# A constant of the tanh moves into the dot, the diagonals for TensorE are half filled ahead of the dot, and the engine of each weighing is chosen at the dot

## The reference

```
s1, i1 = top_k(sc[:, :, 0], 16);  s2, i2 = top_k(sc[:, :, 1], 16)
top_s, pos = top_k(s1[:, None] + s2[None, :], 16);  eid = take(i1 * 128 + i2, pos)
gate = softmax(top_s)
act  = gelu(einsum('cd,chkd->chk', h, u[eid]))            # one dot of 1024 for each token and expert
out  = einsum('chk,chkd->cd', gate * act, v[eid])         # 8 heads x 16 experts = 128 rows of v for each token
```

## Time and profile before

| | |
|---|---|
| median of 3 runs | 3405.8 us (3389.3 to 3409.6) |
| profiled execution, its own time | 3413.8 us |
| its span, first to last instruction | 3412.0 us |
| busy: TensorE / DVE / ACT / GpSimd | 2464.4 / 2574.2 / 1843.8 / 1300.2 us |
| moved by DMA | 1262.32 MB, of it 1086.39 MB by GpSimd's queue |
| granted TensorE clock, mean | 0.842 of full speed |

### The profile page before, as it was taken

The page is one execution under the profiler, slowest core; times in us unless marked ns, Lnnn a source line. Parts: engine busy times, 40 slices in busy tenths (PEclk is TensorE's granted clock), DMA queues, the critical chain, the costliest instruction groups (busy, mean ns, idle before and its releaser), DMA issues.

```text
span 3412.0 us, 34746 instructions
## 1 busy us (share of the span) xinstructions
PE 2464.4 (72%) x7098; PEld 1267.7 (37%) x7098; DVE 2574.2 (75%) x6105; ACT 1843.8 (54%) x6883; POOL 1300.2 (38%) x1044
## 2 busy tenths in 40 slices
PE   7967757898876688877777789868686622666676
PEld 4534434444433344433334344334332200233221
DVE  1267788888978878888778887787876586888854
ACT  1245564455666545566576554556566443455564
POOL 0023343333334534444444433334343344433453
PEclk8988867998976789999886799989898855787899
DMA  7979998899989999999999999999899999898998
GB/s 272 331 308 384 407 352 333 353 408 374 388 345 382 363 376 413 411 403 381 370 369 364 364 397 374 393 373 388 355 386 382 372 364 361 337 385 359 389 407 330
DMA packets 191360, 1262.32 MB, mean 370 GB/s; under 512 B 24849, under 2 KB 32873, under 8 KB 46737
## 3 DMA queue, kind: packets, MB, share of 16 engines
q0 software_dynamic: 149760, 1086.39, 79.7%
q1 hardware_dynamic: 41384, 173.70, 13.6%
HBM read 1251.24 MB, written 43.37 MB: 379 GB/s over the span
## 4 chain that ended last, share of the span: by engine, by line
DMA 30%; PE 25%; DVE 24%; ACT 6%; issue 6%; DVEq 4%; POOL 3%; ACTq 1%; SPq 1%; POOLq 0%
DMA uv_ring<-in_peer_uv,idx 23%; PE acc L1649 12%; DVE uv_ring L2283 9%; DVE accs L2290 5%; POOL uv_ring L1379 3%; PE pS L1438 3%; DMA o_all<-in_cache_swa 2%; PE pS L1557 2%; PE pA L1580 2%; DMA wbuf<-zS_scr 2%; ACT bent L1897 2%; ACT wv L1899 1%; PE acc L1438 1%; PE pS L1490 1%; ACT diag L1699 1%
## 5 line engine op out<-in xcount | busy, mean ns | idle before, releaser
L1379 POOL DMA_INDIRECT uv_ring<-in_peer_uv,idx x1024 | 1283.4, 1253 | 2070.4 <-PE acc L1649 1419.8
L1649 PE MATMUL acc<-uv_ring,diag 128*128 128x512 f32 x2456 | 1338.6, 691 | 493.8 <-ACT diag L1699 479.8
L2283 DVE SCALAR_TENSOR_TENSOR uv_ring<-uv_ring,hb 128x1024 f32<-128x1024 f32 x1032 | 1238.2, 1221 | 368.3 <-DMA uv_ring<-in_peer_uv,idx 348.6
L1649 PEld LDWEIGHTS acc<-uv_ring,diag 128*128 128x128 f32 x2456 | 507.5, 218 | 1169.2 <-ACT diag L1699 611.4
L1884 ACT ACTIVATE cube<-dots 128x1 f32<-128x1 f32 x1032 | 203.5, 197 | 970.9 <-DVE uv_ring L2283 960.5
L2290 DVE SCALAR_TENSOR_TENSOR accs<-uv_ring,wv,accs 128x1024 f32<-128x1024 f32 x410 | 526.7, 1285 | 63.4 <-ACT wv L1899 24.5
L1899 ACT ACTIVATE wv<-bent,half 128x1 f32<-128x1 f32 x1032 | 399.0, 387 | 74.4 <-issue 3.5
L1897 ACT ACTIVATE bent<-dots,line,cube 128x1 f32<-128x1 f32 x1032 | 398.8, 386 | 74.1 <-issue 2.8
L1699 ACT ACTIVATE half<-dots,gates 128x1 f32<-128x1 f32 x1024 | 286.6, 280 | 4.0 <-DVE gates L2175 4.0
L1580 PE MATMUL pA<-T,wbuf 128*128 128x256 f32 (+2 forms) x1280 | 259.4, 360 | 26.3 <-ACT sc L1699 16.1
L1699 ACT ACTIVATE diag<-idn,wv 128x128 f32<-128x128 f32 x614 | 246.5, 401 | 52.0 <-issue 2.1
(11 more groups left out here) (259 smaller groups left out, 2127.3 us busy)
## 6 DMA issues: line engine op xcount, KB each, us to landing
wbuf<-in_w_q SPq DMA_DIRECT2D x40, 1024.0 KB
out_dil_s<-in_cache_dil SPq DMA_DIRECT2D x8, 4092.0 KB
wbuf<-in_w_in SPq DMA_DIRECT2D x26, 1024.0 KB
wbuf<-in_w_out SPq DMA_DIRECT2D x20, 1024.0 KB
uv_ring<-in_peer_uv,idx POOLq DMA_INDIRECT x1024
uv_ring<-in_w_in SPq DMA_DIRECT2D x6, 1024.0 KB, 17.5
keysT<-in_keys SPq DMA_DIRECT2D x40, 128.0 KB
T<-in_xT_all SPq DMA_DIRECT2D x8, 512.0 KB, 13.2
```

The source lines that it names most:

```text
L1379: pool.indirect_dma_start(uv_ring[:, entry % RING, :], None, peer_uv, bass.IndirectOffsetOnAxis(rows, 0))\
L1649: m = pe.matmul(acc[0:R, side * 512:(side + 1) * 512], w, uv_ring[:, entry % RING, D + side * 512:D + (side + 1) * 512], start=first, stop ...
L2283: dve.scalar_tensor_tensor(row, row, 1.0, h, ALU.mult, ALU.mult, accum_out=dots[:, e % RING:e % RING + 1]).then_inc(u_dot, 1)
```

## The change

The dot is multiplied by C at once, so `line` falls away and x itself is the tanh's bias; CUBE and the gates' constant (0.5 becomes 0.5 / C) are adapted. For picks of TensorE, ACT writes identity * gate into the diagonal ahead of the dot ("seed"), the weight is then wv = x * bent + x without `half`, and the diagonal is multiplied by it in place. There are 6 diagonals in place of 4, and the wait for `v_pe` moves from "diag" to "seed". In the planner: the engine of the weighing is chosen when the dot is placed and no longer at the gate's end; "diag" no longer waits for an older weighing, "seed" does, for the one six back; a TensorE pick's gate waits for its seed; the costs and PE_BIAS are other numbers.

```diff
-CUBE = math.sqrt(0.044715 * GELU_C)
+CUBE = math.sqrt(0.044715) / GELU_C
...
-LINES = {"PE": ("weigh",), "ACT": ("gate", "diag", "final"), "DVE": ("weigh", "final", "dot")}
-URGENT = {"gate": 0.4, "diag": 0.5, "weigh": 0.6, "final": 0.7, "dot": 1.0}
+LINES = {"PE": ("weigh",), "ACT": ("gate", "diag", "seed", "final"), "DVE": ("weigh", "final", "dot")}
+URGENT = {"gate": 0.4, "seed": 0.55, "diag": 0.5, "weigh": 0.6, "final": 0.7, "dot": 1.0}
-PE_BIAS = -2.0
+PE_BIAS = -1.0
-GATE = 1.35
+GATE_PE, GATE_DVE = 1.15, 1.45
+DIAGS = 6
...
+                if self.on_pe[p] and u[0] == "f":
+                    return max(self.ends["seed", p], self.ends["dot", p]) if ("seed", p) in self.ends else None
...
+                older = [q for q in sorted(self.on_pe) if self.on_pe[q] and q < p][-DIAGS:1 - DIAGS]
+                if older and len([q for q in self.on_pe if self.on_pe[q] and q < p]) >= DIAGS:
+                    if ("weigh", older[0]) not in self.ends:
+                        return None
...
-            if p not in self.on_pe:
-                self.share(p, gate)
...
             if kind == "diag":
-                older = [q for q in sorted(self.on_pe) if self.on_pe[q] and q < p][-4:-3]
-                if older and ("weigh", older[0]) not in self.ends:
-                    return None
-                return max([gate] + [self.ends["weigh", q] for q in older])
+                return gate
...
+                if kind == "dot":
+                    self.share(p, at + time + GATE_PE)
...
+            def seed(p):
+
+                i = PE_ORD[p]
+                g = gate_of(pick_u(p))
+                if i >= DIAGS:
+                    act.wait_ge(v_pe, i - DIAGS + 1)
+                copy(diag[:, i % DIAGS, :], idn[:, :], g)
+
             def pick_gate(p):
...
+                seeded = ON_PE[p] and u[0] == "f"
                 act.wait_ge(u_dot, e + 1)
                 act.activation(cube[:, c], x, ACT.Square, scale=CUBE)
-                copy(line[:, c], x, GELU_C)
...
+                if not seeded:
+                    copy(half[:, c], x, gate_of(u))
                 act.drain()
-                act.activation(bent[:, c], x, ACT.Tanh, scale=cube[:, c], bias=line[:, c])
+                act.activation(bent[:, c], x, ACT.Tanh, scale=cube[:, c], bias=x)
                 act.drain()
-                act.activation(wv[:, c], bent[:, c], ACT.Identity, scale=half[:, c], bias=half[:, c]).then_inc(g_w, 1)
+                by = x if seeded else half[:, c]
+                act.activation(wv[:, c], bent[:, c], ACT.Identity, scale=by, bias=by).then_inc(g_w, 1)
...
-                if i >= 4:
-                    act.wait_ge(v_pe, i - 3)
-                copy(diag[:, i % 4, :], idn[:, :], w).then_inc(d_set, 1)
+                copy(diag[:, i % DIAGS, :], diag[:, i % DIAGS, :], w).then_inc(d_set, 1)
...
-                dve.scalar_tensor_tensor(row, row, 1.0, h, ALU.mult, ALU.mult,
+                dve.scalar_tensor_tensor(row, row, GELU_C, h, ALU.mult, ALU.mult,
                                          accum_out=dots[:, e % RING:e % RING + 1]).then_inc(u_dot, 1)
```

More of the change, by code:

```diff
@@ L544, in pick_line @@
         if k == "gate":
-            return [("gate", p, GATE) for p in places]
+            return [("gate", p, GATE_DVE) for p in places]
+        if k == "seed":
+            return [("seed", p, 0.42) for p in places if pick_u(p)[0] == "f"]
         return [(kind, t, time) for t in finals for kind, time in
@@ L606, in ready_pick @@
                 at = self.part_end.get((n, len(times_of(BASE[n])) - 1))
+                if self.on_pe[p] and u[0] == "f":
+                    return max(self.ends["seed", p], self.ends["dot", p]) if ("seed", p) in self.ends else None
                 return None if at is None else max(at, self.ends["dot", p])
+            if kind == "seed":
+                if p not in self.on_pe:
+                    return None
+                if not self.on_pe[p]:
+                    self.pick[e, line] += 1
+                    continue
+                u = pick_u(p)
+                n = self.given["g", u[1] // P, u[1] % P // TOPK]
+                at = self.part_end.get((n, len(times_of(BASE[n])) - 1))
+                older = [q for q in sorted(self.on_pe) if self.on_pe[q] and q < p][-DIAGS:1 - DIAGS]
+                if older and len([q for q in self.on_pe if self.on_pe[q] and q < p]) >= DIAGS:
+                    if ("weigh", older[0]) not in self.ends:
+                        return None
+                    at = None if at is None else max(at, self.ends["weigh", older[0]])
+                return at
             if kind == "fsum":
@@ L728, in plan @@
                 kind, p, time = self.picks[e, what][self.pick[e, what]]
+                if kind == "dot":
+                    self.share(p, at + time + GATE_PE)
+                if kind == "gate" and self.on_pe[p] and pick_u(p)[0] == "f":
+                    time = GATE_PE
                 self.pick[e, what] += 1
@@ L848, in build @@
         gates = sb("gates", [P, SLOTS, P])
-        diag = sb("diag", [P, 4, P])
+        diag = sb("diag", [P, DIAGS, P])
         idn = sb("idn", [P, P])
@@ L888, in build @@
         cube = sb("cube", [P, RING])
-        line = sb("line", [P, RING])
         half = sb("half", [P, RING])
@@ L1646, in weigh @@
                 else:
-                    w, R = diag[:, PE_ORD[p] % 4, :], P
+                    w, R = diag[:, PE_ORD[p] % DIAGS, :], P
                 for side in range(2):
@@ L1876, in sample_pT, with gate_of @@
                 copy(s_pTn[0:8, :, :], pT[0:8, 192:320].rearrange("p (s n) -> p s n", s=2)).then_inc(s_bTe, 1)
+            def gate_of(u):
+                if u[0] == "s":
+                    if u[1] == 0:
+                        act.wait_ge(sx_in, 32 * HEADS)
+                    return gateT[:, u[1]:u[1] + 1]
+                t, col = u[1] // P, u[1] % P
+                act.wait_ge(r_gate, GATED[t, col // TOPK])
+                return gates[:, SLOT[t], col:col + 1]
+            def seed(p):
[4 more added lines that the diff above has]
+                copy(diag[:, i % DIAGS, :], idn[:, :], g)
             def pick_gate(p):
@@ L1922, in _ @@
                 if what != "stage":
-                    {"gate": pick_gate, "diag": spread, "fsq": final_squares}[what](s)
+                    {"gate": pick_gate, "seed": seed, "diag": spread, "fsq": final_squares}[what](s)
                     continue
@@ L2174, in gate @@
                 D_()
-                return dve.scalar_tensor_tensor(out, gexp[0:R, c, :], 0.5, gsum[0:R, c].unsqueeze(2)
+                return dve.scalar_tensor_tensor(out, gexp[0:R, c, :], 0.5 / GELU_C, gsum[0:R, c].unsqueeze(2)
                                                 .broadcast_to([R, n, TOPK]), ALU.mult, ALU.mult)
```

## The result

The changed kernel takes 3357.8 us in the median of 4 runs (3350.1 to 3361.8), before 3407.4 us in as many; the ratio is 0.9858 with a 95% interval of 0.9823 to 0.9893, so 1.4% less. The forecast was 3369 us. The profiled execution's own time is 3350.1 us, 63.7 us less than that of before.

What follows compares the result with a forecast made beforehand. Late diagonals, caused by the written order, were taken as the limit, leaving DMA time unused. Order 45 us plus gate 8 us, seeds and choice 0, times 0.7 gave 37 us off 3405.8: 3369 us, range 3326 to 3418.

Steps and rivals of the forecast that it cites:

- What bounds the kernel: Gathers: diagonals filled late by the written order leave about 5% of DMA time, 160 us of 3200, unused.
- Part 1, the gate: ACT's gate: 0.28 us shorter for TensorE picks, 0.10 us for DVE picks; 8 us taken, between 6 and 33.
- the factor 0.7: On the sum of gate and order gains: in three of ten cases another late engine becomes the next wait.
- Part 2, the seeds: ACT: 602 new operations ahead of the dots' ends, mostly covered by waits; 0 taken, up to 9 us loss.
- Part 3, the order: ACT's order: later picks' gates between `wv` and fill fall 354 to 230, 35% of 130 us: 45 us.
- Part 4, the choice: Engine chosen at the dot: 314 picks change engine; 0 taken, 30 us kept both ways for the range.
- (a): Rival at the gathers: the DMA is the bound and nothing moves, 3406 us; chance 0.22.
- (c): Rival on ACT: gates tied to seeds waiting for TensorE stop the ring, slower at 3442 us; chance 0.10.
- (d): Rival: TensorE's late diagonals become late weighings of DVE, eating the gain, about 3395 us; chance 0.12.
- (b): Rival: late diagonals matter more, 54% holds and nothing replaces them, 78 us gain, 3328 us; chance 0.14.
- The signs: Profile after: TensorE's `diag` wait about 300 us, POOL's for TensorE about 1300, DMA share 0.96, ACT busy about 1718.

Runs made afterwards that it cites:

- e4_cost: The kernel before with the planner's gate cost 1.15 instead of 1.35, its choice of engines held fixed, no operation changed: 3361.7 us, ratio 0.9868.
- e1_fold: The kernel before with only the constant moved into the dot and `line` removed; order, choice of engines and four diagonals as before: 3394.0 us, ratio 0.9962.
- e2_ops: All operations of the changed kernel in the order and with the engine choice of the kernel before, each seed directly ahead of its gate: 3399.7 us, ratio 0.9978.
- e3_order: The changed kernel's order, engine choice and six diagonals with the operations of the kernel before (`line`, `half`, no seeds): 3361.8 us, ratio 0.9864.
- e9_next: The kernel before, its operations, engine choice and gate cost kept, with every diagonal fill placed directly behind its own gate: 3325.3 us, ratio 0.9769.
- e10_dve: The kernel before with gate cost 1.15 for DVE's picks alone, 1.35 kept for TensorE's, choice of engines held fixed: 3422.6 us, ratio 1.0054.
- e8_choice_b: The kernel before with the changed kernel's choice of engines held fixed, gate cost 1.35 kept, order planned anew: 3446.3 us, ratio 1.0103.
- e5_first: The changed kernel with every diagonal fill placed directly behind its own gate, engines chosen as the changed kernel does: 3319.2 us, ratio 0.9749.
- e12_simple: e9_next plus e1_fold: every fill right behind its gate, constant in the dot, no `line`, four diagonals, no seeds: 3323.4 us, ratio 0.9726.
- e13_seeds: e9_next plus e2_ops: every fill right behind its gate, with all operations of the changed kernel and six diagonals: 3319.7 us, ratio 0.9730.

## Why the prediction was right, and where it was not

**What bounds the kernel: right.** Late diagonals leave the DMA without work. Read from two stretches and the table of waits before the run, it held in the experiments: with the fills prompt the rate goes from 376 to 387 GB/s, with them later it falls to 371.

**Who makes them late: wrong.** The prediction said that the planner held the fills back until a weighing four picks older had ended. That rule holds nothing back: the planner of before writes the same order with a rule on four or on six picks back, or with none. What decides is the gate's cost. The planner spaces the dots of picks that lie ready by 1.31 (the cost of "dot" in `pick_line`), and with a gate of 1.35 the next gate is always due when one ends, ahead of the fill, which is due HOP = 0.15 later. With 1.15 there is room for the fill. The planner shows both steps when e4_cost's kernel is planned with other costs: at 1.309 there are 45 fills behind two or more gates and at 1.31 there are 85; at 1.159, just below 1.31 - 0.15, there are 175 later gates ahead of fills and at 1.16 there are 296. In the changed planner a cost of 1.35 for TensorE's gates, all else as changed, gives 391 later gates and not 230. That the number makes the order and the order the time is shown by e4_cost. The forecast did not suffer from this mistake, by luck: its counts, 354 and 230, were taken from the written orders, whoever made them. On the chip the next dot often comes later than in the plan, and ACT, which runs in order, waits for it with the fill behind it.

**Part 1, the gate.** `bent` starts 0.26 us after `cube` for a seeded pick (944.90 to 945.16 in the timeline), as worked out. The term was 8 us, 6 after the factor 0.7. e1_fold, with the smaller part of the cut alone, gave 13 us, e2_ops with all of it 8 us, with intervals as wide as the difference. In the changed kernel's order all the operations together gave 2 us (e3_order against the changed kernel). The term stands within what can be measured.

**Part 2, the seeds: right** in that they cost nothing on the path, and this is why they win nothing: they remove 0.18 us more from a gate and add an operation of 388 ns.

**Part 3, the order: right mechanism, sized too low.** 45 us x 0.7 = 32 us were forecast, e3_order gave 1.36% of 3407 = 46 us, and e4_cost, without the new choice, 1.32% = 45 us. That the sum of the forecast came near owes something to the cut of 0.7: the same price, 130 us for all the later gates, gives 67 us for e4_cost, which removes 52% of them, and 130 us for e9_next, which gave 79 us. There the factor fits, 0.67 and 0.61; for the changed kernel it was not needed. The number of later gates is a rough measure, and the fills behind two or more are no better one: e10_dve and e8_choice_b have fewer of these than before and are slower.

**Part 4, the choice: 0 taken.** With before's costs and an order planned around it, it costs 1.0% or 35 us, a little over the 30 us that were kept; in the new order it may win up to 0.5%.

**The rivals.** (a), the DMA as the bound: the limit of about 358 GB/s from HBM that the Trainium skill gives in "DMA: Bandwidth & Descriptors", section "Where 436 GB/s comes from", does not hold for this core, which moves 384 GB/s as the mean of 3100 us and 387 in e9_next. Its reads from HBM alone are 1251 MB by the page of the changed kernel, 374 GB/s over the whole span of 3348 us. (c), a seed that blocks ACT: 2.6 us with four diagonals. (d), late weighings of DVE in place of TensorE's: POOL's waits for DVE grew by 34 us, over a third of what those for TensorE fell; it took a part and not the gain. (b), the larger case, did not come for the change; a time like its 3328 us is what the prompt order of e9_next reached, at 3325 us.

**The signs.** The share of 0.96 and POOL's stop below 8 us at the head came true; POOL's 1329 us against about 1300 nearly. TensorE's wait for `diag` was to fall to 300 us and stayed at 472. That step failed: with every fill prompt it is still 470 (e9_next) and 435 us (e5_first), so its sum is no measure of the delay. The likely reason, not shown, is that a slot freed sooner brings the pick behind it sooner too, and that TensorE, faster than the gathers, always waits for some pick. ACT's busy time was to be 1718 us and is 1805.8. There the sum of durations misled, for these operations lie partly on top of their neighbours. Taking `line` out lowered ACT's busy time by 92 us from the kernel before to e1_fold, 0.09 us each and not 0.19. `half` overlaps its neighbour by about as much as `line` does, so of its 0.28 us 0.19 go. From e12_simple to e13_seeds, where 614 seeds replace as many `half`, ACT's busy time rises by 63 us, from 1748.2 to 1811.0, so a seed adds about 0.29 us and not 0.40. With these the sum is 93 + 114 - 175 + 5 = 37 us less, and 38 were measured. The prediction had named 0.31 us for a seed and then counted 0.401.

## What to carry to other kernels

Where an order is written ahead of time, look on each in-order engine for short operations that release a buffer and stand behind an operation that waits for something else: the difference between the start of the producer and the start of that operation, 9.46 us here, is the figure to read. Such a delay, summed over the picks, followed the time of the kernels better than any count in the plan, and moving the operation up can be worth more than making the operations shorter. A planner's cost that is a few hundredths above or below a neighbour's cost can flip such an order throughout; ask which comparisons are near to equal before the costs are measured more finely. And a wait that is always there on an engine with time to spare says little on the path: TensorE's for the diagonal was 472 us in the changed kernel and 470 in e9_next. One line of the waits of the engine that feeds the bound is no sure measure either. POOL waited 65 us less for TensorE in e10_dve than before, and that kernel is slower; it waited 102 us less in e4_cost than in the changed kernel, at the same time. Its waits for TensorE and DVE together come nearer to the times: 1750 us before, 1693 in the changed kernel, 1680 in e4_cost and 1587 in e9_next.

## What the runs showed of the hardware

An ACT operation on 128x1 takes 187 ns with constants, 280 ns with one operand of 128x1 as scale and 386 ns with scale and bias, but back to back the next one starts 0.09 to 0.10 us after a 187 ns one. The filled diagonal takes 402 ns in place, as it took from the identity (401 ns). With 1 MB gathers the core moved 415 GB/s in a full stretch and 387 GB/s as the mean of 3100 us, more than had been expected from the 376 of before.
